# Delta layers: rows of the cumulative decays and of beta by transposes of a stride-zero column

## The reference, cut to what matters

```python
aq, ak, av = _l2norm(heads_a(aq)), _l2norm(heads_a(ak)), heads_a(av)
beta = jax.nn.sigmoid(a_b)
g = -jnp.exp(dn_a_log) * jax.nn.softplus(a_a + dn_dt_bias)
...
G = jnp.cumsum(g, axis=-1)
gamma = jnp.exp(jnp.where(incl, G[..., :, None] - G[..., None, :], -jnp.inf))
kb = k * beta[..., None]
a_kk = jnp.where(strict, jnp.einsum('bhnid,bhnjd->bhnij', kb, k) * gamma, 0.0)
...                               # (I + a_kk) is inverted and applied
qk = jnp.einsum('bhnid,bhnjd->bhnij', q, k) * gamma
```

## Time and profile before

| | |
|---|---|
| median of 3 runs | 2207.88 us (2206.93 to 2209.4) |
| span of the profiled execution | 2207.0 us (its time around the span is not listed apart) |
| PE busy | 2173.5 us, 98% |
| DVE busy | 1727.9 us, 78% |
| ACT busy | 1434.2 us, 65% |
| mean granted clock of TensorE | 0.998 |

### The profile page before, as it was taken

The page is one execution under the profiler, slowest core; times in us unless marked ns, Lnnn a source line. Parts: engine busy times, 40 slices in busy tenths (PEclk is TensorE's granted clock), DMA queues, the critical chain, the costliest instruction groups (busy, mean ns, idle before and its releaser), DMA issues.

```text
span 2207.0 us, 30890 instructions
## 1 busy us (share of the span) xinstructions
PE 2173.5 (98%) x11392; PEld 1811.0 (82%) x11392; DVE 1727.9 (78%) x1980; ACT 1434.2 (65%) x1597; POOL 64.2 (3%) x96
## 2 busy tenths in 40 slices
PE   9999999999999999999999999999999999999999
PEld 6788897778888888888888887779978898988888
DVE  6766656688888888888888889867668886776887
ACT  6644444767777777777778776656565556565654
POOL 3000000020000000000000003000000000000000
PEclk9999999999999999999999999999999999999999
DMA  9755555279999999999999999843135554224551
GB/s 385 287 190 183 182 189 192 105 278 387 358 396 365 394 372 387 371 378 374 374 389 364 390 367 391 322 189 117 68 140 194 182 200 151 83 106 155 189 187 62
DMA packets 83523, 573.26 MB, mean 260 GB/s; under 512 B 9744, under 2 KB 10368, under 8 KB 18224
## 3 DMA queue, kind: packets, MB, share of 16 engines
q1 hardware_dynamic: 77760, 545.29, 64.8%
q0 software_dynamic: 5376, 26.12, 3.2%
q10 hardware_dynamic: 288, 0.52, 0.1%
HBM read 564.03 MB, written 17.83 MB: 264 GB/s over the span
## 4 chain that ended last, share of the span: by engine, by line
PE 89%; DVE 5%; ACT 4%; issue 1%; DMA 1%; SPq 0%; ACTq 0%; POOL 0%; DVEq 0%; POOLq 0%
PE bank L831 65%; PE bank L899 10%; PE bank L901 5%; DVE w_lo L542 2%; ACT w_hi L537 2%; PE bank L1190 1%; PE bank L1315 1%; PE bank L1325 1%; ACT arena L1532 1%; PE bank L1230 1%; PE bank L800 1%; DMA raw<-in_wu_qkv 1%; PE bank L954 0%; DVE arena L2089 0%; ACT L537 0%
## 5 line engine op out<-in xcount | busy, mean ns | idle before, releaser
L542 DVE TENSOR_TENSOR w_lo<-raw,w_hi 128x2048 fp32r<-128x2048 f32 x505 | 1156.3, 2300 | 253.1 <-ACT w_hi L537 251.5
L537 ACT CAST w_hi<-raw 128x2048 fp32r<-128x2048 f32 x505 | 963.6, 1912 | 343.4 <-PE bank L831 260.8
L831 PE MATMUL bank<-w_hi,xT 128*128 128x512 f32 x2368 | 754.6, 393 | 4.3 <-DVE w_lo L542 3.4
L831 PEld LDWEIGHTS bank<-w_hi,xT 128*128 128x128 f32 x2368 | 445.1, 188 | 111.3 <-DVE w_lo L542 12.1
L831 PE MATMUL bank<-w_lo,xT 128*128 128x512 f32 x1184 | 461.8, 390 | 0.0
L831 PE MATMUL bank<-w_hi,aT_hi 128*128 128x512 f32 x864 | 344.4, 399 | 2.3 <-DVE w_lo L542 2.3
L899 PE MATMUL bank<-xT,w_hi 128*128 128x512 f32 x960 | 340.1, 398 | 0.8 <-issue 0.4
L831 PE MATMUL bank<-w_hi,aT_lo 128*128 128x512 f32 x864 | 337.3, 390 | 0.0
L831 PE MATMUL bank<-w_lo,aT_hi 128*128 128x512 f32 x864 | 336.6, 390 | 0.0
L901 PE MATMUL bank<-xT,w_lo 128*128 128x256 f32 x960 | 269.4, 281 | 0.0
L831 PEld LDWEIGHTS bank<-w_lo,xT 128*128 128x128 f32 x1184 | 222.8, 188 | 44.2 <-issue 0.5
(11 more groups left out here) (350 smaller groups left out, 1721.2 us busy)
## 6 DMA issues: line engine op xcount, KB each, us to landing
raw<-in_wu_eg SPq DMA_DIRECT2D x112, 1024.0 KB, 7.2
raw<-in_wu_eu SPq DMA_DIRECT2D x112, 1024.0 KB, 7.3
raw<-in_wu_ed SPq DMA_DIRECT2D x112, 1024.0 KB, 7.3
raw<-in_wu_up SPq DMA_DIRECT2D x44, 1024.0 KB, 4.8
raw<-in_wu_ffn_gu SPq DMA_DIRECT2D x28, 1024.0 KB, 4.8
raw<-in_wu_in SPq DMA_DIRECT2D x28, 1024.0 KB, 4.8
raw<-in_wu_down SPq DMA_DIRECT2D x22, 1024.0 KB, 4.8
raw<-in_wu_ffn_d SPq DMA_DIRECT2D x14, 1024.0 KB, 4.8
```

The lines of the kernel that those rows point to most:

```text
L537: nc.scalar.copy(w_hi[:, place(i), :], src).then_inc(*E.hi.mark("unit", i))
L542: nc.vector.tensor_tensor(w_lo[:, place(i), :], raw[:, i % RAW, :], w_hi[:, place(i), :].bitcast(F32), ALU.subtract) \
L831: mm = nc.tensor.matmul(o, l[i], r[j], start=(first and n == 0), stop=(last and n == 2), skip_group_check=not lone)
```

## The change

The float32 products of `grow` and `brow` become transposes. A new helper gives PE a column of a small tile, read 128 times over with stride zero, to be transposed with the identity: the result has the column's 128 values along the free dimension of every partition. For `grow` the column is of `ngc` (the negated running sum, from ACT), so DVE's two operations that used the rows turn an addition into a subtraction; for `brow` it is of `brk`. The two `spread` copies on DVE and their tiles go away. `grow` moves on PE from before `project(2, 0)` to between its two halves, and waits for `ngc` (the release of bank 7); `brow` waits for `brk`. The diff, without the part that renames the tiles `gB` and `bB` to `AT` and `qk`, which lived in them later anyway:

```diff
+                def rows_of(col, t):
+                    return lambda dst, h: nc.tensor.transpose(dst, col[:, t, h:h + 1].to_broadcast([P, P]), ident)
...
-                pe.wait_ge(*decay.at(L, "gB"))
-                for t in range(NT):
-                    heads(open_bank(M, 4 + t), "grow", t, product(lambda h: dn["gB"][:, t * DN_H + h, :], lambda h: C("upto")))
                 for j in range(2):
                     open_bank(M, j)
-                project(2, 0)
-                pe.wait_ge(*decay.at(L, "bB"))
-                for t in range(NT):
-                    heads(open_bank(M, 2 + t), "brow", t, product(lambda h: dn["bB"][:, t * DN_H + h, :], lambda h: ident))
+                project(2, 0, (0,))
+                pe.wait_ge(*M.free[7].at("gcol", L))
+                for t in range(NT):
+                    heads(open_bank(M, 4 + t), "grow", t, rows_of(ngc, t))
+                project(2, 0, (1,))
+                pe.wait_ge(*decay.at(L, "brk"))
+                for t in range(NT):
+                    heads(open_bank(M, 2 + t), "brow", t, rows_of(brk, t))
...
-                def spread(dst, src, key):
-                    V_.tensor_copy(dst, src.rearrange("p a b -> p (a b)").unsqueeze(2).to_broadcast([P, N_DN, P])) \
-                        .then_inc(*decay.mark(L, key))
...
-                ve.wait_ge(*decay.at(L, "g"))
-                spread(dn["gB"], gl, "gB")
...
-                chain(V_.tensor_tensor(brk, rk, beta, ALU.mult))
-                spread(dn["bB"], brk, "bB")
+                V_.tensor_tensor(brk, rk, beta, ALU.mult).then_inc(*decay.mark(L, "brk"))
...
-                        V_.tensor_tensor(kdsc, gr[:, :, P - 1], ngc[:, 0, :], ALU.add).then_inc(*decay.mark(L, "last"))
-                    V_.tensor_tensor(dn["gam"][:, t * DN_H:(t + 1) * DN_H, :], gr,
-                                     msk[:, LEVELS * P:(LEVELS + 1) * P].unsqueeze(1).to_broadcast([P, DN_H, P]), ALU.add) \
+                        V_.tensor_tensor(kdsc, ngc[:, 0, :], gr[:, :, P - 1], ALU.subtract).then_inc(*decay.mark(L, "last"))
+                    V_.tensor_tensor(dn["gam"][:, t * DN_H:(t + 1) * DN_H, :],
+                                     msk[:, LEVELS * P:(LEVELS + 1) * P].unsqueeze(1).to_broadcast([P, DN_H, P]), gr, ALU.subtract) \
                         .then_inc(*M.free[4 + t].mark("grow", L, t))
...
+                ve.wait_ge(*decay.at(L, "brk"))
```

More of the change, by code:

```diff
@@ L281, in build_program @@
         att["sg"] = Rf.rearrange("p (a n) -> p a n", n=512)
-        dn = carve(0, [("cv", (12, S)), ("z", (NT, 512)), ("gB", (N_DN, P)), ("bB", (N_DN, P)),
+        dn = carve(0, [("cv", (12, S)), ("z", (NT, 512)), ("AT", (N_DN, P)), ("qk", (N_DN, P)),
                        ("gam", (N_DN, P)), ("kb", (DN_H, S)), ("DT", (N_DN, P)), ("Xl", (N_DN, P))])
@@ L289, in build_program @@
         dn["D"] = dn["gam"]
-        dn["AT"] = dn["gB"]
-        dn["qk"] = dn["bB"]
         dn["u"] = dn["LT"]
```

## The result

The changed kernel is slower: 2215.68 us median (2212.76 to 2219.7, 6 runs) against 2209.31 us (2206.93 to 2211.09, 6 runs) for the kernel before, a ratio of 1.0031 with a 95% interval of 1.0021 to 1.0041. That is 6.4 us more, where 1.7 us more was forecast (against 2207.88), and it lies above the range, which ended at 2212.5. All six times of the changed kernel lie above all six of the kernel before. One slow run of the kernel before (3109 us at a mean clock of 0.646, one of the 33 whose median is 2208.79) is left out of the ratios. The profiled execution took 2215.58 us, 1.8 us more than its span of 2213.8 us; the span before was 2207.0.

What follows compares the result with a forecast made beforehand. PE, busy 98% of the span, bounds the kernel. 3.64 us saved, 3.6 waited, 0.1 late; minus 1.6 for the old fall, plus 3.2 for two new: +1.7, giving 2209.6 us, range 2204.5 to 2212.5.

Steps and rivals of the forecast that it cites:

- The saving on PE: `grow` and `brow` as transposes 0.109 us apart save 0.91 us a group, 3.64 us over four groups.
- DVE's wait before `last`: DVE stands 0.9 us for the moved `grow` before L2456, making `last` 0.31 us later.
- ACT's wait 0.3 us longer: ACT's wait for `last`, which DVE writes at L2456, grows by 0.3 us.
- PE's wait for the square: Before the sums of squares of the queries PE idles 1.8 us for ACT's square, using up the layer's savings.
- The clock: PE's 1.8 us idle plus 1.7 us of one-column products lets the clock fall, three chances in four at each new place.
- a fall at each new place: Falls behind the wait for the square in both delta layers, 1.6 us each, plus 3.2 us in the sum.
- minus 1.6 us for the fall of this profile: The fall behind the sums of the keys and gcol goes away; one chance in four that it stays.
- The bound at the upper end: Range ends at 2212.5 us, holding three falls but short of four; slower than 2212.3 had chance 0.08.
- The rival on the slower side: The clock falls at all four places, old and new, 1.6 us each, giving 2212.8 us; chance 0.08.
- The sign that the prediction gave for itself: Prediction wrong if PE shows no idle, or time moves over 4 us, unless transposes are slow.
- case (B): PE waits for the square but the clock holds at the new places, 2206.4 to 2208.0 us; chance 0.17.

Runs made afterwards that it cites:

- fill: Changed kernel with two idle float32 products of 512 columns on PE before its wait for the square of the queries; 2209.57 us against 2208.84, ratio 1.0002.
- wait alone: Changed kernel, wait for the square kept, narrow products behind it moved past a quarter of the next projection; 2209.34 us against 2209.06, ratio 0.9998.
- grow only: Changed kernel with `brow` as float32 products of a spread column again, `grow` still transposes between the projection's halves; 2209.34 us against 2208.84, ratio 1.0008.
- brow only: Kernel before with only `brow` turned into transposes of `brk`, `grow` left alone; 2208.03 us against 2208.84, ratio 0.9997.
- narrow twice: Kernel before with the sixteen narrow products of the queries issued twice, second set unused, no wait; 2214.64 us against 2209.06, ratio 1.0028.
- sums later: Changed kernel with the wait and sums of squares of the queries behind a quarter of the next projection; 2208.27 us against 2208.84, ratio 1.0001.

## Why the prediction was wrong

**Right, point by point.** The saving on PE: eight transposes in 1.03 us, 0.109 us apart, and no price for the stride-zero operand. DVE's wait before `last`: 0.9 us forecast, 0.99 measured (2.47 in the first layer, where the fall at the old place came). ACT's wait 0.3 us longer: 0.35. PE's wait for the square: 1.8 us forecast, 1.72 in both layers, so that the sums come no earlier: from gcol to them 15.61 us before and 15.65 after in the second layer (forecast: the same), 17.18 and 17.13 in the first. The fall of the clock behind it: in both layers, shown to be the cause by the fill (the fall goes, and the 6 us with it) and by "wait alone" (the wait with the narrow products moved away brings none).

**The step that failed** is the one called "The clock", and its term in the sum: "a fall at each new place, 1.6 us each by the earlier trace rows". The mechanism was right and the size was off. The fall cost 3.3 us in each layer, because it lasted 6.8 us and not the 3.4 us of the only falls that the rows had: 6.6 us instead of 3.2. The second part of the term, "minus 1.6 us for the fall of this profile", did not come either; in the profile after, the old fall is there again at the same place. The prediction gave one chance in four to that, since wide products now follow gcol; of the fourteen stages of kernels with this order seven had the fall, which is no fewer than the one in two of before. That the two profiles agree in it is luck of the draw. With these two put right the sum is 6.6 + 0.1 = 6.7 us on the span, and 6.8 was measured.

The bound at the upper end had the same fault. It counted falls, up to four, and gave all of them the one price of the rows; what bounded the price from above, a fall of another length, was not asked. The rival on the slower side, which needed four falls, got 0.08. The sign that the prediction gave for itself, a move of more than 4 us "which nothing in these stretches can carry", came true: two long falls carry it. Its chances don't agree either: three in four for a fall at each of two places leave one in sixteen for none, yet that case (B) got 0.17.

A smaller part of the miss is the base. Of the 6.1 us between 2209.6 and 2215.68, 1.4 lie between the 2207.88 us of three runs of the kernel before and the 2209.31 us of six.

## What to carry to other kernels

When PE is made faster between two points that another engine's chain ties together, work out what PE will wait for, and then what the wait does to the clock: here 3.6 us of saving became 3.4 us of idle time and 13.6 us at half speed, which cost 6.6 us. In "wait alone" a wait of 1.7 us brought no fall, and neither did 1.7 us of one-column products between wide ones or behind `brow` in the other profiles; next to each other the two cost 3.3 us. So it is worth keeping such products away from waits, between wide products. And price a fall of the clock by more than one case, since its length is not fixed.

## What the runs showed of the hardware

In the twelve traces every fall that the end of the span does not cut off lasted 3.4 or 6.8 us. In the three long ones of the delta layers, two of the changed kernel and one of "grow only", the clock fell while PE was still in the quiet place (at 1526.2, 1898.3 and 1894.7 us): the narrow products themselves slowed, from 1.84 or 1.95 to 2.63, 2.74 and 2.51 us. The traces have two more long falls, outside the delta layers: in "brow only" the clock fell at 1425.6, 2.0 us before a wait of PE ended, and in "grow only" at 1423.7, 0.7 us before one did. The short falls began when PE had other work again, as in "narrow twice", where the narrow products had ended by 1528.0 and the clock fell at 1529.3, or within 0.2 us of that ("fill" at 1426.7, "sums later" at 1508.3). So the long fall went with a quiet place that lasted on after the clock had fallen. That this sets the length was not tried by itself and stays open.

The clock fell behind 3.4 us of one-column products although the profile calls PE busy there, and it did not fall behind eight or twenty-four float32 transposes with 1.7 us of such products after them. Transposes did not always keep it up, though: in a layer that the change does not touch, the clock fell while eight transposes ran (L802, at 1437.1 us in "narrow twice") behind a wait of 2.33 us.
